# A transformer layer in split-float matmuls: buffer starts rounded to 64 bytes, an early read-back, and one split moved behind eight adds

## What is computed

```python
up = _dwconv3(_rmsnorm(x, norm2) @ w_up, conv_w, conv_b)      # 2 * 2816 columns
gate, val = up[..., :D_FF], up[..., D_FF:]
x = x + (jax.nn.silu(gate) * val) @ w_down
g = jax.nn.sigmoid(_rmsnorm(x, norm3) @ w_ple_gate + b_ple_gate)
x = x + (p @ w_ple_proj) * g
```

## Time and profile before

| | us |
|---|---|
| median of 3 runs (1349.06 to 1350.76) | 1350.56 |
| the profiled execution | 1346.59 |
| its span, first to last instruction | 1344.8 |
| PE busy in it | 1280.2 (95%) |
| DVE busy | 750.6 (56%) |
| ACT busy | 463.9 (34%) |
| POOL busy | 161.5 (12%) |
| mean granted clock of TensorE, share of full | 0.983 |

### The profile page before, as it was taken

The page is one execution under the profiler, slowest core; times in us unless marked ns, Lnnn a source line. Parts: engine busy times, 40 slices in busy tenths (PEclk is TensorE's granted clock), DMA queues, the critical chain, the costliest instruction groups (busy, mean ns, idle before and its releaser), DMA issues.

```text
span 1344.8 us, 15892 instructions
## 1 busy us (share of the span) xinstructions
PE 1280.2 (95%) x5487; PEld 979.7 (73%) x5487; DVE 750.6 (56%) x1107; ACT 463.9 (34%) x744; POOL 161.5 (12%) x139
## 2 busy tenths in 40 slices
PE   5899699999999999999999999999799999999996
PEld 4687455555588788888888888888688888877885
DVE  5547786786447665555545454545333365336664
ACT  4312465565412342323232323232222244224333
POOL 0137400000065300000000000000000011002100
PEclk8999799999999999999999999999899999999999
DMA  5420000010334222222222222222244443432332
GB/s 177 174 55 13 8 10 0 10 31 1 129 122 125 63 63 78 63 78 62 78 62 78 62 78 62 78 62 94 95 137 145 138 142 139 143 117 84 112 112 92
DMA packets 116107, 113.38 MB, mean 84 GB/s; under 512 B 6291, under 2 KB 98794, under 8 KB 115306
## 3 DMA queue, kind: packets, MB, share of 16 engines
q1 hardware_dynamic: 115776, 112.84, 26.0%
q10 hardware_dynamic: 298, 0.11, 0.0%
HBM read 93.01 MB, written 19.92 MB: 84 GB/s over the span
## 4 chain that ended last, share of the span: by engine, by line
PE 81%; DVE 6%; issue 1%; ACT 1%; DVEq 0%; ACTq 0%
PE ps L188 25%; PE ps L190 25%; PE ps L189 25%; PE ps L520 3%; PE ps L508 2%; DVE XT L1234 1%; DVE SF L1211 1%; DVE XT L1214 1%; DVE XT L1210 1%; DVE col L1227 0%; DVE WDHL L1220 0%; DVE WL L201 0%; DVE TL L1455 0%; PE ps L407 0%; DVE GHL L1222 0%
## 5 line engine op out<-in xcount | busy, mean ns | idle before, releaser
L188 PE MATMUL ps<-XH,WH 128*128 128x512 f32 x1096 | 441.5, 403 | 3.7 <-DVE SF L1126 3.7
L189 PE MATMUL ps<-XL,WH 128*128 128x512 f32 x1096 | 435.9, 398 | 0.0
L190 PE MATMUL ps<-XH,WL 128*128 128x512 f32 x1096 | 435.7, 398 | 0.0
L201 DVE TENSOR_TENSOR WL<-WR,WH 128x1024 fp32r<-128x1024 f32 (+2 forms) x137 | 174.0, 1273 | 209.9 <-ACT WH L196 209.8
L196 ACT ACTIVATE WH<-WR 128x1024 fp32r<-128x1024 f32 (+2 forms) x137 | 139.6, 1020 | 343.6 <-PE ps L190 334.8
L188 PEld LDWEIGHTS ps<-XH,WH 128*128 128x128 f32 x1096 | 207.6, 189 | 57.3 <-DVE WL L201 4.5
L189 PEld LDWEIGHTS ps<-XL,WH 128*128 128x128 f32 x1096 | 207.4, 189 | 51.3 <-issue 2.2
L190 PEld LDWEIGHTS ps<-XH,WL 128*128 128x128 f32 x1096 | 207.3, 189 | 50.6
L961 ACT ACTIVATE SF<-SF,col 128x512 f32<-128x512 f32 x88 | 71.7, 816 | 305.4 <-DVE SF L1329 305.4
L1329 DVE TENSOR_TENSOR SF<-ps,R 128x512 f32<-128x512 f32 x88 | 60.5, 689 | 185.5 <-PE ps L190 179.9
L188 PE MATMUL ps<-GHL,WH 128*128 128x512 f32 x352 | 140.3, 399 | 6.9 <-DVE GHL L1375 6.9
(11 more groups left out here) (151 smaller groups left out, 1250.7 us busy)
## 6 DMA issues: line engine op xcount, KB each, us to landing
WR<-in_w_up SPq DMA_DIRECT2D x44, 512.0 KB, 3.8
WR<-in_w_down SPq DMA_DIRECT2D x44, 512.0 KB, 3.5
g_scratch<-SF SPq DMA_DIRECT2D x22, 512.0 KB, 2.8
SF<-g_scratch SPq DMA_DIRECT2D x44, 256.0 KB, 3.6
WR<-in_w_out SPq DMA_DIRECT2D x16, 512.0 KB, 3.9
WR<-in_w_ple_gate SPq DMA_DIRECT2D x16, 512.0 KB, 3.8
WR<-in_w_in SPq DMA_DIRECT2D x8, 512.0 KB, 3.9
xt_scratch<-XT SPq DMA_DIRECT2D x2, 2048.0 KB, 12.6
```

The costliest lines, as they stand in the source:

```text
L188: pe.matmul(out, wh, xh, start=first, stop=False)
L189: pe.matmul(out, wh, xl, start=False, stop=False)
L190: return pe.matmul(out, wl, xh, start=False, stop=last)
L201: dve.tensor_tensor(WL[:, slot(n), base:cols, :], WR[:, slot(n), base:cols, :], WH[:, slot(n), base:cols, :].bitcast(F32), ALU.subtract).t ...
```

## The change

Three sizes are rounded up to multiples of 16 floats (`par` 215 to 224, `col` 172 to 176, `SF` 5124 to 5136), so that every buffer starts on a multiple of 64 bytes. The read-back of activated tiles 0 and 1 goes from the end of up to the place behind pair 1 on SP; the two copies on ACT and the two subtractions on DVE go behind the pair with index 2, the third. For that, pairs 1 and 2 become straight code on ACT and DVE, and pair 1 on SP. On DVE, the rest of gate tile 1 goes behind all eight adds of sequence 1.

```diff
+LINE = 16
-        par = sb("par", [P, NPAR])
+        par = sb("par", [P, LINE * -(-NPAR // LINE)])
-        col = sb("col", [P, CP + 32])
-        SF = sb("SF", [P, 5124])
+        col = sb("col", [P, LINE * -(-(CP + 32) // LINE)])
+        SF = sb("SF", [P, LINE * -(-5124 // LINE)])
...
-            with sp.Fori(1, NPAIR) as i:
+            def up_pair(i):
                 load_up(i, 0)
                 store_g(i - 1, 0)
...
+            up_pair(1)
+            for c in range(2):
+                sp.wait_ge(g_out[c], 16)
+                load_g(0, 0, c, first=True)
+            with sp.Fori(2, NPAIR) as i:
+                up_pair(i)
             load_down(0, 0, 0)
             store_g(NPAIR - 1, 0)
             load_down(0, 0, 1)
-            for c in range(2):
-                sp.wait_ge(g_out[c], 16)
-                load_g(0, 0, c, first=True)
             load_down(0, 0, 2)
...
-            with act.Fori(1, NPAIR) as i:
-                mlp(i)
...
+            mlp(1)
+            mlp(2)
+            g_split(0, 0)
+            g_split(0, 1)
+            with act.Fori(3, NPAIR) as i:
+                mlp(i)
...
-            g_split(0, 0)
-            g_split(0, 1)
             with act.Fori(0, FT // 2 - 1) as q:
...
-            with dve.Fori(1, NPAIR) as i:
-                mlp(i, False)
...
+            mlp(1, False)
+            mlp(2, False)
+            g_low(0, 0)
+            g_low(0, 1)
+            with dve.Fori(3, NPAIR) as i:
+                mlp(i, False)
...
-            g_low(0, 0)
-            g_low(0, 1)
             with dve.Fori(1, FT // 2) as q:
...
             split_w_lo(dve, T_GATE, T_GATE)
-            for m in range(2):
+            for m in range(KT):
                 add_down(KT + m)
             split_w_lo(dve, T_GATE + 1, T_GATE + 1)
-            for m in range(2, KT):
-                add_down(KT + m)
```

More of the change, by code:

```diff
@@ L957, in convolve @@
                         act.wait_ge(silu_done, r + 1)
-                    elif f or not isinstance(i, int):
+                    elif f or not isinstance(i, int) or i:
                         act.wait_ge(g_ready, r - 1)
@@ L965, in convolve @@
                         act.wait_ge(conv_done, t + 1)
-                        if s == 0 and not isinstance(i, int):
+                        if s == 0 and (not isinstance(i, int) or i):
                             act.wait_ge(g_out[f], i * 16)
@@ L1326, in scaled @@
                 dve.wait_ge(up_ready, t + 1)
-                if c or not isinstance(i, int):
+                if c or not isinstance(i, int) or i:
                     dve.wait_ge(conv_done, t - 1)
```

## The result

The changed kernel takes 1326.03 us in the median (1323.81 to 1329.01, 4 runs), beside 1349.81 (1346.54 to 1350.76, 4 runs) for the kernel before: a ratio of 0.983, 95% interval 0.980 to 0.986. The forecast was 1318 with a range of 1303 to 1341. The range held, but the likeliest value missed by 8 us.

A forecast was written before the change was run, and what follows sets the result against it. The prediction took PE, busy 95% of the span, as the bound. Gains of 6.5 + 6.0 + 19.5 = 32.0 us off the profiled 1346.6 gave 1314.6, or 1318 for the runs' median, range 1303 to 1341.

The forecast's parts named there:

- Part A: Start of down, early read-back: 5.9 us earlier start, 2.5 from the clock, less 1.9 new wait; 6.5 us, between 4.0 and 8.5.
- The clock stays whole there: Start of down: the short idle left should not drop PE's clock to 1.2 GHz, saving 2.46 us more.
- The new wait: Some 11 us into down: PE waits 1.9 us for tile 2's read-back, queued on SP behind a load and a store.
- The reading of the next wait: Down, tile 1: weights ready at 955.97, just before tile 0 ends at 956.4, so nothing stops there.
- Rival 4: Start of down also waits for tile 1's split, so the early read-back gives under 1 us; chance 0.05 within each case.
- Part B: Between down and gate, split behind the adds: gate starts 4.1 us earlier, whole clock saves 1.9; 6.0 us together.
- The cover behind the moved split: Start of gate: the diagonal, at about 1211.5, comes before PE wants it at 1213.4, two us of cover.
- Part C: All ring matmuls, buffers on 64 bytes: 4344 matmuls 4.5 ns closer, 19.5 us, with bounds 0 and 35 us.
- the scores of attention: Attention row with both operands on 64 bytes: 389 ns at least but 396 in the median, evidence against the full gain.
- Rival 1: Ring matmuls: the spacing stays, only the early read-back and moved split count, 12.5 us, giving 1338; chance 0.30.
- Rival 2: Ring matmuls: every one gains the whole 8 ns step, 35 + 12.5 us, giving 1303; chance 0.14.
- Rival 3: Ring matmuls: PE's two reads meet on the same large multiple, 17.4 us lost less 12.5, giving 1355; chance 0.06.

The follow-up runs named there:

- e1: The changed kernel without the three size roundings, so early read-back and moved split alone: 1338.89 us, ratio 0.991 to the kernel before.
- e12: e4 with the pad ahead of all buffers grown by 8 floats, every start 32 bytes past a multiple of 256, distances kept: 1308.86 us, ratio 0.969.
- e5: e4 with WH and WL alone moved 64 bytes past a multiple of 256, every buffer still on 64: 1338.03 us, ratio 0.992.
- e4: The changed kernel with all of PE's operands on multiples of 256 bytes, by padding ahead of XT and in par: 1306.92 us, ratio 0.968.
- e6: e4 with GHL, the moving operand of down, alone moved 64 bytes past a multiple of 256: 1310.05 us, ratio 0.971.
- e7: e4 with the read-back of activated tiles 2 and 3 ahead of the loads of down tiles 2 and 3 on SP: 1304.86 us, ratio 0.967.
- e10: e4 with the pad ahead of all buffers grown by 16 floats, every start 64 bytes past a multiple of 256: 1307.14 us, ratio 0.969.
- e11: e4 with the pad ahead of all buffers grown by 32 floats, every start 128 bytes past a multiple of 256: 1307.50 us, ratio 0.969.
- e3: The changed kernel with WH and WL alone pushed 32 bytes past a multiple of 64: 1337.87 us, ratio 0.991 to the kernel before.

## Why the prediction was right and where it was wrong

**Part A: right, term by term.** PE's idle before down shrank from 6.85 to 0.78 us, 6.1 (forecast 5.9). The clock stays whole there (2.5). That step came right with luck: the row that it was read from, PE busy 2.35 us of 6.0 and the clock whole, is one that no other execution profiled here repeats, as the last section shows. The new wait is 1.94 us (forecast 1.9), for the reason given: tile 2's read-back went out at 953.78 behind the loads and the store, and the copy that waits for it starts 5.5 us later. The reading of the next wait was too generous by a hair: tile 1's weights were ready at 951.68 + 1.22 = 952.90 where tile 0 ends at 947.58 + 24 x 0.2267 = 953.02. The cover of 0.4 us that I had counted was 0.1. Rival 4 is out: PE started at 947.58, over 5 us before those weights were ready.

**Part B: right.** 12.7 - 6.7 = 6.0 us, forecast 6.0. The cover behind the moved split held: the diagonal is done at 1194.32 + 0.88 = 1195.20 and the broadcast's matmuls start at 1197.18, two us later as counted.

A and B together were 12.5; e1 shows 10.9 by the medians, and 12.5 lies in its interval.

**Part C: the range held, the size and the reason did not.** I took 4.5 ns for each of 4344 matmuls, 19.5 us. Measured are 12.9 us (e1 to after), 3.0 ns on average: 233.3 - 226.7 = 6.6 ns in down (1056 matmuls, 7.0 us), 1.9 in up (2112, 4.0), about 1 in the gate (384 and 96 small ones, 0.5); the 1.4 us left are within the spread of the medians. With the 1.6 us that A and B are short by the medians, the missing 6.6 make the 8 us between 1318 and 1326.

The step that failed is the sentence "a matmul whose next weights lie on 64 bytes can be 8 ns shorter". It was read from one difference between two rows: the small products had their weights on a multiple of 64, and 389 ns, the others 32 past, and 397. Its size was read from a third of the small products. The row with 389 is the first matmul of each three in `mm3`; all three lines in before are

```profile
L188 PE MATMUL ps<-CHL,WDHL x32: 387/389/400, 1218.0 to 1329.8; 128*128 128x512 f32 x32
L189 PE MATMUL ps<-CHL,WDHL x32: 387/393/398, 1218.3 to 1330.0; 128*128 128x512 f32 x32
L190 PE MATMUL ps<-CHL,WDHL x32: 387/396/400, 1218.5 to 1330.3; 128*128 128x512 f32 x32
```

and the spacing inside these blocks of six is 230.1 ns in the mean, 4 under up's 234.3, not 8. The block that the prediction shows, at 1225.90, is one of the four fast ones (226.7); the other twelve have 230.2 to 232.0.

The reason was wrong too, for the rows differ in a second thing that I didn't work out: `CHL` and `WDHL` lie a multiple of 512 bytes apart, `XH` and `WH` 160 past one. e12 has no start on 64 and all of the step, e5 all starts on 64 and nothing of it in down (233.3) and 1 ns in up. The change brings its 12.9 us because the rounding happens to make the distance of `GHL` and `WH` a multiple of 512, and that of `XH` and `WH` 128.

For a short block the distance isn't the whole account. `CHL` and `WDHL` keep theirs in every run, and yet all their blocks run at 226.7 ns only where the gate's `XH` by `WH` matmuls just before them do (e4, e6, e7, e10, e11, e12); in the other runs the mean of the blocks is 229.5 to 231.5. In e4:

```profile
L190 PE MATMUL ps<-CHL,WDHL x32: 389/389/389, 1180.7 to 1289.6; 128*128 128x512 f32 x32
```

So what a block of six shows depends on the stream before it, and such a row could not have given the price of a stream of thousands. Why it does was not tried.

The other row that I weighed, the scores of attention with 396 in the median, has that distance too (`WDHL`, `GHL`), and doesn't answer to it: in e6, where it is 192 instead of 0, the spacing of neighbouring scores is 232.3 ns, beside 232.0 in e4. These products use 96 of the 128 partitions and come in short blocks; which of the two counts, no run shows.

**The rivals.** Rival 1 (spacing stays, 1338) had the price right, as e1 shows at 1338.9, but with the roundings the spacing moved. Rival 2 (every matmul gains, 1303) was right on the price: e4 gains 32.0 us over e1 and comes to 1306.9. Only it isn't this change that reaches it. Rival 3 had the sign wrong: it feared that PE's reads meet when both operands start on the same large multiple, and that is the fastest case.

The Trainium skill, page "SBUF — State Buffer", section "Specifications (TRN2)", gives SBUF lines of 16 bytes; by it a start 32 bytes off costs nothing. e12 agrees for the start by itself (226.7 ns at 32 past). That page of the Trainium skill says nothing of two operands at once, and there the measurement decides: 32 bytes between them cost 6.6 ns a matmul (down of e3). The Trainium skill's page "TensorE: Matmul & The Clock Gate", section "Step-by-step: what each phase is for", comes nearer: PE has two independent read ports for the two operands, and loading the next weights takes nothing from the running matmul. If nothing else held PE up, the distance would not matter by it; the table above shows 226.7 to 234.3 ns for the same instructions. Whether it is at the ports that the operands meet, no run here shows.

**The start of the kernel** lost 1.5 us (154.3 to 155.8) that no part had. Its place is the last section's.

## What to carry to other kernels

Where PE is the bound and every matmul has new weights, compare the spacing of matmuls by stage and by pair of operands, and look at the difference of the two start addresses, not at each of them: here a distance of a multiple of 512 bytes was worth 32 us of 1339 (e1 to e4), for a few hundred bytes of padding per partition. Read a price from a long stream, not from a short block. Before a row is taken as evidence for a cause, write down everything in which it differs from the row beside it. When a step is moved ahead of a stall, follow the transfers of the next tiles as well: here the stall came back as 1.9 us, and moving two transfers took it away.

## What was unexpected of the hardware

Besides the distance, one thing. Early on PE waits 3.7 us for DVE, in both kernels alike (the earlier trace rows and the page's lines above), and the clock behind that wait is not the same. The window 55 to 60 us in before, then in after:

```profile
55.00:60.00 5.00, 4.16 (x18) 3.41 (x19) 4.80 (x8) 1.15 (x2) 0.00 (x0) 1.00 0.54 167
```
```profile
55.00:60.00 5.00, 4.37 (x10) 3.48 (x11) 4.77 (x8) 1.14 (x2) 0.00 (x0) 0.50 0.59 180
```

The clock is 1.00 in the one and 0.50 in the other. All other executions profiled here show 0.50 to 0.67 in that window, e1 with the layout of before among them. So the profile of before was a favourable one in this place, which fits its time (1346.59) lying 3.2 us under its median of 1349.8, and from the end of that wait to PE's next idle of over 1.5 us it is 75.2 us in before and 77.6 in after. The first stage takes 153.4 to 157.8 us in the twelve experiments, 157.4 in e1, so as far as these runs show, its 1.5 us are no cost of the change. What decides it was not tried.
